# GpSimd sums the squares, wider openings and half-slot splits in a six-stage TensorE kernel

## The reference

```
h = rms_norm(x) * g_pre            # mean over the 1024 channels of x*x
y = layer(h)                       # projections h @ w_in, a mixer, @ w_out
x = x + rms_norm(y) * g_post
```

## Time and profile before

| what | value |
|---|---|
| median of 3 runs | 1914.7 us (1914.07 to 1916.35) |
| span of the profiled execution, first to last instruction | 1915.6 us |
| busy: PE, DVE, ACT, POOL | 1770.9, 926.6, 758.6, 950.2 us |
| mean granted clock of TensorE | 0.966 |
| first product (L660) of the openings of odd, diff, ffn0, ssm, ffn1 | 322.90, 604.13, 880.96, 1256.58, 1527.38 us |

### The profile page before, as it was taken

How to read it: one execution, slowest core, us unless ns; L and a number is a source line. 1 busy time by engine, 2 the same in 40 slices (tenths; PEclk the granted TensorE clock), 3 DMA queues, 4 the chain that set the end, 5 groups by cost and what they waited for, 6 DMA issues and landing times.

```text
span 1915.6 us, 20168 instructions
## 1 busy us (share of the span) xinstructions
PE 1770.9 (92%) x7526; PEld 1337.8 (70%) x7526; DVE 926.6 (48%) x1394; ACT 758.6 (40%) x1261; POOL 950.2 (50%) x1108
## 2 busy tenths in 40 slices
PE   9999989999989889789999999998889899999996
PEld 6766557677767666466888888865445678888885
DVE  2043435666836799526632413357547544032344
ACT  4264554365464324644332322343333542222231
POOL 4433124457944454024655556569124456565662
PEclk9999999999999999799999999999879999999998
DMA  5221112222102221012322332311001223333231
GB/s 201 86 64 61 33 45 87 66 67 77 56 23 88 66 77 56 2 54 89 95 94 97 100 99 93 97 54 55 11 12 33 67 69 96 99 99 98 90 99 66
DMA packets 39697, 139.90 MB, mean 73 GB/s; under 512 B 4528, under 2 KB 4656, under 8 KB 39472
## 3 DMA queue, kind: packets, MB, share of 16 engines
q1 hardware_dynamic: 39600, 138.61, 22.6%
HBM read 136.50 MB, written 2.10 MB: 72 GB/s over the span
## 4 chain that ended last, share of the span: by engine, by line
PE 76%; DVE 11%; ACT 7%; POOL 3%; issue 2%; DMA 0%; SPq 0%; ACTq 0%; DVEq 0%; POOLq 0%
PE ps L643 18%; PE ps L645 17%; PE ps L644 17%; DVE ps L1882 2%; PE ps L706 2%; PE ps L683 2%; POOL wl L2811 2%; PE ps L685 2%; PE ps L684 2%; PE ps L663 1%; PE ps L669 1%; PE ps L660 1%; PE ps L1281 1%; PE ps L959 1%; ACT wh L741 1%
## 5 line engine op out<-in xcount | busy, mean ns | idle before, releaser
L2811 POOL TENSOR_TENSOR wl<-raw,wh 128x256 fp32r<-128x256 f32 x988 | 813.6, 854 | 842.0 <-ACT wh L741 836.3
L741 ACT ACTIVATE wh<-raw 128x1024 fp32r<-128x1024 f32 x246 | 259.9, 1057 | 559.2 <-PE ps L645 499.8
L643 PE MATMUL ps<-hh,wh 128*128 128x512 f32 x1068 | 437.2, 409 | 13.7 <-POOL wl L2811 3.6
L645 PE MATMUL ps<-hh,wl 128*128 128x512 f32 x1068 | 418.7, 392 | 0.0
L644 PE MATMUL ps<-hl,wh 128*128 128x512 f32 x1068 | 418.6, 392 | 0.0
L643 PE MATMUL ps<-mh,wh 128*128 128x512 f32 x632 | 261.7, 414 | 19.2 <-DVE ml L1910 4.0
L643 PEld LDWEIGHTS ps<-hh,wh 128*128 128x128 f32 x1068 | 202.4, 190 | 71.7 <-issue 13.6
L645 PE MATMUL ps<-mh,wl 128*128 128x512 f32 x632 | 250.4, 396 | 0.0
L644 PE MATMUL ps<-ml,wh 128*128 128x512 f32 x632 | 250.0, 396 | 0.0
L644 PEld LDWEIGHTS ps<-hl,wh 128*128 128x128 f32 x1068 | 202.7, 190 | 45.6 <-issue 6.0
L645 PEld LDWEIGHTS ps<-hh,wl 128*128 128x128 f32 x1068 | 202.0, 189 | 43.0
(11 more groups left out here) (477 smaller groups left out, 2443.2 us busy)
## 6 DMA issues: line engine op xcount, KB each, us to landing
raw<-in_w SPq DMA_DIRECT2D x246, 512.0 KB, 3.5
x<-in_x SPq DMA_DIRECT2D x8, 256.0 KB, 7.5
out<-x SPq DMA_DIRECT2D x8, 256.0 KB, 2.0
arena<-in_rope SPq DMA_DIRECT2D x3, 512.0 KB, 3.9
arena<-in_dec SPq DMA_DIRECT2D x1, 1024.0 KB, 7.7
mats<-in_mats SPq DMA_DIRECT2D x1, 576.0 KB, 8.5
raw<-in_w SPq DMA_DIRECT2D x2, 256.0 KB, 3.8
arena<-in_lw SPq DMA_DIRECT2D x1, 512.0 KB, 4.0
```

The source lines that it names most:

```text
L643: e.matmul(ps[b][:], a, xh, start=first, stop=False)
L645: e.matmul(ps[b][:], l, xh, start=False, stop=final).then_inc(pe.sem, pe.up(*step))
L741: e.activation(wh[:, n % NHL, :], raw[:, n % NRAW, :], ACT.Copy).then_inc(rounded.sem, rounded.up(n))
L2811: e.tensor_tensor(wl[:, n % NHL, cut(i, 2)], raw[:, n % NRAW, cut(i, 2)], wh[:, n % NHL, cut(i, 2)].bitcast(F32), SUB).then_inc(split.sem, ...
```

## The change

- `OPENS`: the openings of odd, diff, ffn0, ffn1 and ssm take four groups a block in place of three (two in ssm). The groups that come in no longer stand behind the opening; banks are dealt anew where needed.
- Outside `even`, ACT writes the squares to the eight blocks of `y`, and no longer waits for TensorE. POOL adds squares 1 to 6 onto square 0, one instruction a block (step `sa`). TensorE then needs two float32 matmuls against ones in place of eight, at the end.
- The transposes for `rcol` leave `rs` for a step of their own, `rt`, which stands later in even, odd and diff and nowhere in the other stages. DVE waits for `rb_pre` alone before the steps `e`.
- A slot is split by two POOL instructions of four tiles in place of four of two; the first three slots keep four. Waits by part follow.
- In `odd` `lm` uses the banks 6, 7, 2, 3, `gl` the banks 4, 5, 0, 1; `rt` stands behind gl0. In `diff` e(ub1) and its product `um` stand ahead of the convolution. In `ssm` the two groups su0 and su1 are what is left behind the opening, and the norms stand behind them.

```diff
@@ opening
         out += [("w", g, k) for g in gs]
-        out += [("sq", n) for n in (SQUARES.get(k, ()) if gs == tuple(OPENS["even"]) else (k,))]
-    return out + [("rs",)]
+        if gs == tuple(OPENS["even"]):
+            out += [("sq", n) for n in SQUARES.get(k, ())]
+        elif 1 <= k < KT - 1:
+            out.append(("sa", k))
+    return out + ([] if gs == tuple(OPENS["even"]) else [("sq", KT - 1)]) + [("rs",)]
-OPENS = {"even": [("sq", 0), ("sq", 1), ("sq", 2)], "odd": [("lx", 0), ("lx", 1), ("lx", 2)],
-         "diff": [("ua", 0), ("ub", 0), ("ua", 1)], "ffn0": [("fg", 0), ("fu", 0), ("fg", 1)], "ssm": [("cq", 0), ("cq", 1)]}
+OPENS = {"even": [("sq", 0), ("sq", 1), ("sq", 2)], "odd": [("lx", 0), ("lx", 1), ("lx", 2), ("lx", 3)],
+         "diff": [("ua", 0), ("ub", 0), ("ua", 1), ("ub", 1)], "ffn0": [("fg", 0), ("fu", 0), ("fg", 1), ("fu", 1)],
+         "ssm": [("cq", 0), ("cq", 1), ("ckv", 0), ("kr", 0)]}
@@ steps_odd
-    out += group(lx[3], 8, ("bd", 2), ("lc", 0), ("e", lx[3]), ("bd", 3))
-    out += merge(groups([("gl", j) for j in range(4)], 8, "e", "gm"), lru)
+    gl = groups([("gl", j) for j in range(4)], 8, "e", "gm")
+    out += gl[:8] + [("rt",)] + merge(gl[8:], lru)
@@ steps_diff
-    out = opening(*OPENS["diff"]) + [("e", ("ub", 0)), ("lb",), ("e", ("ua", 0)), ("um", 0), ("e", ("ua", 1)), ("tb",)]
-    out += merge(u[1], conv[:8]) + merge(v, conv[8:34]) + merge(u[2] + u[3], conv[34:78]) + [("le",)]
+    out = opening(*OPENS["diff"]) + [("e", ("ub", 0)), ("lb",), ("e", ("ua", 0)), ("um", 0), ("e", ("ua", 1)), ("tb",),
+                                     ("e", ("ub", 1)), ("um", 1), ("rt",)]
+    out += merge(v, conv[:34]) + merge(u[2] + u[3], conv[34:78]) + [("le",)]
@@ steps_ssm
-    out = opening(*OPENS["ssm"]) + [("an", 0), ("e", c[0]), ("e", c[1])]
-    out += group(c[2], 8, ("e", c[2]), ("nq", 0), ("ns", 0), ("an", 1))
-    out += group(c[3], 8, ("nq", 1), ("e", c[3]), ("nk", 0), ("an", 2))
-    out += group(c[4], 8, ("nk", 1), ("e", c[4]), ("ka", 0))
-    out += group(c[5], 8, ("e", c[5]), ("kb", 0))
+    out = opening(*OPENS["ssm"]) + [("an", 0), ("e", c[0]), ("e", c[1]), ("e", c[2])]
+    out += group(c[4], 8, ("nq", 0), ("ns", 0), ("an", 1), ("nq", 1), ("e", c[3]), ("nk", 0))
+    out += group(c[5], 8, ("nk", 1), ("e", c[4]), ("ka", 0), ("an", 2), ("e", c[5]), ("kb", 0))
@@ pe_norms
+            elif kind == "sq" and stage != "even":
+                claim(e, 7)
+                e.wait_ge(s.pool.sem, s.pool["sa", KT - 2])
+                e.matmul(ps[7][:], M("ones"), y[:, 0, :], start=True, stop=False)
+                e.wait_ge(act.sem, act["square", KT - 1])
+                e.matmul(ps[7][:], M("ones"), y[:, KT - 1, :], start=False, stop=True).then_inc(pe.sem, pe.up("sq", KT - 1))
+                busy[7] = (act, ("rb_pre_ln",))
@@ act_norms, kind "hi"
-                at = square_at(stage)
-                if k >= len(at):
-                    e.wait_ge(pe.sem, pe["sq", k - len(at)])
-                e.activation(at[k % len(at)], x[:, k, :], ACT.Square).then_inc(act.sem, act.up("square", k))
+                if stage == "even" and k >= len(square_at):
+                    e.wait_ge(pe.sem, pe["sq", k - len(square_at)])
+                to = square_at[k % len(square_at)] if stage == "even" else y[:, k, :]
+                e.activation(to, x[:, k, :], ACT.Square).then_inc(act.sem, act.up("square", k))
@@ new
+        def pool_norms(e, stage, step):
+            act, pool = S[stage].act, S[stage].pool
+            if step[0] == "sa":
+                k = step[1]
+                e.wait_ge(act.sem, act["square", k])
+                if k > 1:
+                    e.wait_ge(pool.sem, pool["sa", k - 1])
+                e.tensor_tensor(y[:, 0, :], y[:, 0, :], y[:, k, :], ADD).then_inc(pool.sem, pool.up("sa", k))
@@ split_slot
-            for i in range(0, SLOT, 2):
+            many = parts_of(n)              # 2 for the first three slots, 4 for the others
+            for i in range(0, SLOT, many):
@@ pool_program
                     if (stage, step) in STARTS and 0 < STARTS[stage, step] <= NSLOT - NHL:
                         split_slot(e, STARTS[stage, step] + NHL - 1)
+                    pool_norms(e, stage, step)
```

More of the change, by code:

```diff
@@ L165, in steps_even @@
     sq, sk = ([(g, j) for j in range(4)] for g in ("sq", "sk"))
-    out = opening(*OPENS["even"]) + merge(group(sq[3], 8), [("e", g) for g in sq[:3]]) + [("e", sq[3])] + groups(sk, 8, "e")
+    out = opening(*OPENS["even"]) + merge(group(sq[3], 8), [("e", g) for g in sq[:3]]) + [("e", sq[3]), ("rt",)] + groups(sk, 8, "e")
     out += [("t", "sv", k) for k in range(8)] + [("te", "sv", i) for i in range(4)]
@@ L201, in steps_odd @@
     lx = [("lx", j) for j in range(4)]
-    out = opening(*OPENS["odd"]) + [("e", lx[0]), ("e", lx[1]), ("bd", 0), ("bd", 1), ("e", lx[2])]
-    out += group(lx[3], 8, ("bd", 2), ("lc", 0), ("e", lx[3]), ("bd", 3))
+    out = opening(*OPENS["odd"]) + [("e", lx[0]), ("e", lx[1]), ("bd", 0), ("bd", 1), ("e", lx[2]), ("bd", 2), ("lc", 0), ("e", lx[3]),
+                                    ("bd", 3)]
     lru = []
@@ L293, in steps_ffn @@
             elif f == 1:
-                mul = merge(group(u, 8), pend)
+                mul = pend
             else:
@@ L463, in bank, with parts_of @@
     return of[g[-1] % len(of)]
+def parts_of(n):
+    return 2 if n < NHL else 4
 class Signal:
@@ L606, in program @@
         sqr = [nrm[:, 2, :], nrm[:, 3, :]]
-        def square_at(stage):
-            return sqr + [nrm[:, 4, :], nrm[:, 5, :]] if stage == "even" else sqr
+        square_at = sqr + [nrm[:, 4, :], nrm[:, 5, :]]
         rcol = little(4)
@@ L639, in product @@
                     e.wait_ge(split.sem, split["wl", n])
-            elif i % 2 == 0:
-                e.wait_ge(split.sem, split["wl", n] if i + 2 == SLOT else split["part", n, i])
+            elif i % parts_of(n) == 0:
+                e.wait_ge(split.sem, split["wl", n] if i + parts_of(n) == SLOT else split["part", n, i])
             a, l = tile(stage, step)
@@ L666, in open_products @@
                 n, i = divmod(PLACE[stage, step], SLOT)
-                if i % 2 == 0 or (k, g) == (KT - 1, gs[-1]):
-                    e.wait_ge(split.sem, split["wl", n] if i + 2 >= SLOT or (k, g) == (KT - 1, gs[-1]) else split["part", n, i])
+                if i % parts_of(n) == 0 or (k, g) == (KT - 1, gs[-1]):
+                    whole = i + parts_of(n) >= SLOT or (k, g) == (KT - 1, gs[-1])
+                    e.wait_ge(split.sem, split["wl", n] if whole else split["part", n, i])
                 e.matmul(ps[bank(stage, g)][:], tile(stage, step)[1], hh[:, k, :], start=False, stop=(k == KT - 1)).then_inc(
@@ L696, in pe_norms @@
             pe, dve, act = s.pe, s.dve, s.act
-            if kind == "sq":
+            if kind == "sa":
+                pass
+            elif kind == "sq" and stage != "even":
[5 more added lines that the diff above has]
+                busy[7] = (act, ("rb_pre_ln",))
+            elif kind == "sq":
                 k = step[1]
@@ L700, in pe_norms @@
                     claim(e, 7)
-                    if stage == "even":
-                        e.wait_ge(s_mats, 16)
-                if stage == "even" and k == KT - 1:
+                    e.wait_ge(s_mats, 16)
+                if k == KT - 1:
                     e.wait_ge(consts.sem, consts[EXACT[-1]])
                 e.wait_ge(act.sem, act["square", k])
-                e.matmul(ps[7][:], M("ones"), square_at(stage)[k % len(square_at(stage))], start=(k == 0), stop=(k == KT - 1)).then_inc(
+                e.matmul(ps[7][:], M("ones"), square_at[k % len(square_at)], start=(k == 0), stop=(k == KT - 1)).then_inc(
                     pe.sem, pe.up("sq", k))
+                if k == KT - 1:
+                    busy[7] = (act, ("rb_pre_ln",))
             elif kind == "rs":
+                pass
+            elif kind == "rt":
+                claim(e, 7)
                 e.wait_ge(act.sem, act["rb_pre"])
@@ L808, in dve_norms @@
             elif kind == "rs":
+                e.wait_ge(act.sem, act["rb_pre"])
+            elif kind == "rt":
                 e.wait_ge(pe.sem, pe["rcol"])
                 e.tensor_copy(rcol, fours(ps[7][:])[:, :, 0]).then_inc(dve.sem, dve.up("rcol"))
-                e.wait_ge(act.sem, act["rb_pre"])
             elif kind == "oe":
@@ L1557, in act_odd @@
                     e.wait_ge(pe.sem, pe["lm", j, i])
-                    e.activation((rr, ig)[i][:, j, :], ps[4 + (2 * j + i) % 4][:], ACT.Sigmoid, scale=1.0,
+                    e.activation((rr, ig)[i][:, j, :], ps[LMB[(2 * j + i) % 4]][:], ACT.Sigmoid, scale=1.0,
                                  bias=V(("ba", "bx")[i], j)).then_inc(act.sem, act.up("lm", j, i))
@@ L2807, in split_slot @@
             e.wait_ge(rounded.sem, rounded[n] if n else rounded["half"])
-            for i in range(0, SLOT, 2):
+            many = parts_of(n)
+            for i in range(0, SLOT, many):
```

(5 more changed lines are left out.)

4 lines of the change are left out of this document (2 added, 2 removed), and 8 rows, old and new, of the table BANKS.

## The result

The changed kernel takes 1929.7 us (median of 1928.09, 1929.74 and 1932.09; a fourth run, at 2905 us and a mean granted clock of 0.554, was disturbed and is left out). The kernel before took 1914.4 us beside it: ratio 1.0083, interval [1.0064, 1.0102], 16 us slower. Forecast were 1895 us and a gain of 20 us.

What follows compares the result with a forecast made beforehand. TensorE was taken to bound the kernel, with DVE and POOL limiting the openings; even 1.3, odd 1.3 + 1.7, diff -1.4, ffn0 3.7, ssm 7.0 and ffn1 6.6 sum to 20.2 us, giving 1895 us, range 1881 to 1909.

Steps and rivals of the forecast that it cites:

- Halves: POOL saves 0.6 us a slot; in an ffn worth nothing, in odd 1.7 us gained: Slot splits: two POOL halves at 1.1 us replace 2.83 us; some 10 slots in odd save 6 us, 1.7 counted.
- rival E: Slot splits: a half costs as much as two quarters (1.42 us), p 1.75; 1910 us; chance 0.07.
- they go by turns, one pair in a time p = 1.54: Openings: POOL's 14 wide instructions alternate with DVE's, needing 14 x 1.54 = 21.6 us, plus about 2 us standing still.
- Rival D: Openings: DVE and POOL in turns bound them; p of 2.0 costs 31 us, giving 1926 us; chance 0.07.
- ffn0: Stage ffn0: squares done 3.7 us later than before, yet TensorE gains 3.7 us as the fourth group moves inside.
- ffn1: Stage ffn1: three splits, not four, start before the sixth sum; opening ends at 1552.4, not 1559.0: 6.6 us gained.
- diff: Stage diff: DVE's taps start with the factor 3.7 us later, less 0.3 and about 2 us of waits: loss 1.4 us.
- odd: Stage odd: 4.16 us of DVE's wait and 0.8 for `rcol` go, `rb_pre` comes 3.7 later: 1.3 us gained, halves aside.
- ssm: Stage ssm: two groups go into the opening; the group un starts at 1299.2, not 1306.19: 7.0 us gained.
- even: Stage even: 1.84 us of wait gone, less 0.45 for the transposes further back: 1.3 us gained.
- B: Openings run at TensorE's floor (pairs at 1.2 us or less), end squares waiting for nothing: 38.4 us gained, 1876 us; chance 0.14.
- The wait at 424.50: Odd: TensorE's wait for the chain of DVE's convolutions and LRU, 3.12 us before, should be longer than before.

Runs made afterwards that it cites:

- quarters_again: The changed kernel with every slot split by four POOL instructions again, sums on POOL and wide openings kept: 1916.6 us, ratio 1.0018 to the kernel before.
- wide_openings_alone: The changed kernel with halves and POOL's sums both undone (quarters, squares on TensorE), wide openings kept: 1908.8 us, ratio 0.9973 to the kernel before.
- wide_but_in_diff: Wide openings alone, but diff as in the kernel before (three groups, old order and banks): 1904.4 us, ratio 0.9955 to the kernel before.
- halves_alone: The kernel before with the halves alone: 1931.7 us, ratio 1.0097 to the kernel before.
- combined kernel: Quarters, wide openings but in diff, squares summed by DVE in ffn0, ssm and ffn1: 1900.2 us, ratio 0.9923 to the kernel before.
- eighths_alone: The kernel before with a slot split by eight POOL instructions of 128 columns: 1915.1 us, ratio 1.0009 to the kernel before.
- halves_behind_openings: The kernel before with halves, but quarters for slots that POOL splits during an opening: 1928.1 us, ratio 1.0075 to the kernel before.
- squares_on_pe: The changed kernel without POOL's sums, TensorE doing one square matmul per block, halves and wide openings kept: 1918.8 us, ratio 1.0030 to the kernel before.
- sums_alone: The kernel before with POOL's sums alone (quarters, three groups, two in ssm): 1942.2 us, ratio 1.0154 to the kernel before.

## Why the prediction was wrong

Of the forecast gain of 20.2 us, 1.7 stood for the halves and 18.5 for the openings with their sums. The halves cost 13.1 us in the changed kernel (1929.7 against 1916.6), which is most of its loss. All the rest, measured by quarters_again, lost 3.4 us (1916.6 against 1913.2). So both terms failed: by about 15 us the first, by about 22 us the second. Of these 22 the sums on POOL are 7.8; most of the others are ssm (7.0 forecast, 1.4 with wide openings alone) and ffn1 (6.6 forecast, 2.2).

**Step "Halves: POOL saves 0.6 us a slot; in an ffn worth nothing, in odd 1.7 us gained".** This step failed, and it makes a loss out of the change. POOL's saving is half of what was assumed (a quiet slot takes 2.54 us, against 2.83: a half is 1.27, not 1.1). The other side was not in the sum at all: outside the openings I priced the halves on POOL only, in the forecast and in rival E. There the longer DVE instructions hold TensorE up: in the kernel's time the halves cost 18.5 us alone, 9.9 with wide openings, 13.1 with the sums too. The earlier trace rows had the mechanism in view, I used it for the openings only, and the earlier trace rows had the price of 512 columns.

**Step "they go by turns, one pair in a time p = 1.54".** This was near the mark. POOL's 14 instructions ran from 889.37 to 915.50 with 4.0 us of standing still: (26.1 - 4.0) / 14 = 1.58, where true pairs take 1.6 to 1.7. I took 2 us of standing still. The 2 us missing there and 14 x 0.04 are why the sixth sum ends 31.3 us after the first scaling (915.50 - 884.19) and not 28.7 (907.4 - 878.67). Rival D, which said 1926 us, had p at 2.0 and its point at 1.84: its number came near and its reason was wrong.
The Trainium skill's "SBUF — State Buffer", section "Who interferes with whom", has it that the loser waits for a whole instruction of the other, without sharing bandwidth. The runs agree in that DVE's wait grows with the width of POOL's instruction (0.83, 1.11, 1.66 us), and in the strict turns. I had set the rule aside because a quarter's 0.71 + 0.61 us was more than the 1.11 seen; but 0.71 is the shown duration, and turns of 1.14 us leave POOL 0.53 of them. By the same sum a half has 1.65 - 0.61 = 1.04 us of its 1.27, twice as much for twice the width. So the rule holds if the pair is held for somewhat less than the shown duration; that is an estimate from the spacing, and no run shows the hold itself.

**The sums themselves.** The forecast weighed them against the openings of before, never against wide openings with the squares left on TensorE. By its own numbers those end after 2.3 + 8 x 3.58 = 30.9 us, and with the sums at 30.4: half a microsecond for 30 new instructions. Measured, the last square of ffn0 starts at 30.9 us without the sums and 32.4 with them beside halves, at 30.8 and 32.8 beside quarters; the sums cost 7.8 us beside quarters, 11.0 beside halves, 29 alone.

**Stage by stage.** *ffn0* and *ffn1* were to give 3.7 and 6.6 us, and gave 0.9 and 0.2; wide openings alone give 2.0 and 2.2. In ffn1 three splits did come before the sixth sum, but the first of them began 9.2 us after the first scaling (1544.94 - 1535.74), not 5.2 as in ffn0: the last square starts after 31.6 us, where an end at 27.3 was forecast. *diff*, forecast -1.4, is -5.9: the mechanism (taps on DVE that start late) was right, as wide_but_in_diff shows, and its size too small: the taps start 6.7 us later after the first scaling, not 3.4. *odd*: the 4.16 us of DVE's wait were to pay for the late factor. Wide openings alone gain 1.4 there, within the scatter of that column; with the halves it is a loss of 3.2, with the sums too of 4.2. *ssm*: 7.0 us were to come by the earlier start of un. It came 2.9 us earlier (1307.98 - 1258.97 = 49.0 after the first scaling, before 51.9 by the earlier trace rows), and 8.9 us were lost behind it: 3.7 up to the attention's first scores and 4.3 in the attention (139.9 us from its first scores to its last, before 135.6), which is as long in halves_alone. Nor did an early start of un pay by itself: in wide_openings_alone it comes 4.7 us earlier and the stage gains 1.4. The combined kernel starts it 5.4 us earlier and gains 7.1.

*even*: the mechanism was right; its size, 1.3 us, is below what the even column can tell. At the end of its opening, first the kernel before, then the changed one:

```profile
34.95 0.66 PE L711 MATMUL ps<-mats,nrm 128*128 128x128 f32 x4 [1.44 <-ACT nrm L766]
35.36 0.48 PE L643 MATMUL ps<-hh,wh 128*128 128x512 f32 x1
```

```profile
31.25 1.02 PE L722 MATMUL ps<-nrm,mats 128*128 128x512 f32 x2
31.71 0.79 PE L650 MATMUL ps<-hh,wh 128*128 128x512 f32 x1
```

The product follows the square at once.

**The signs named.** The wait of the end squares for POOL was 0.54 us, neither the 1 us of the forecast nor the nothing of B; TensorE had by then waited 4.9 us for DVE's `hl`, which the forecast did not have. From the first scaling to f = 2's first product it was 32.9 us, not 30.4. DVE's instructions took 1.66 to 1.78 us beside a half, not 1.5, and quiet halves 1.27, not 1.1. The wait at 424.50 grew to 3.67 us, as said. In diff the 5.43 us went, as said, but the wait at 692.52 stayed (2.74, then 2.68 us) and two others came ahead of it. The mark "wrong if ffn0 and ffn1 together give under 6 us" was met.

**Left open.** How much of ssm's loss is a chain, how much the phase in which splits meet DVE's instructions, and how much TensorE's clock (below). Beside wide openings, sums alone or halves alone leave ssm at a gain (2.3 and 1.8), both together lose 6.0; in the kernel before, halves lose 5.3 there and sums 9.8. And odd lies between -3.6 and +0.2 in three kernels whose code is the same there.

## What to carry to other kernels

Price an instruction's width on the engine that shares its operands' memory as well as on its own: fewer, wider instructions on POOL saved it 112 us of work here (halves_alone) and cost DVE 77. Work put on a half-idle engine is not free when its result stands behind that engine's queue and a chain waits for it. And weigh each part against the best kernel without it, not against the kernel before.

## What the runs showed of the hardware

A DVE addition of two SBUF operands (512 columns, 0.69 us) lasts 0.83, 1.11 or 1.66 us beside a POOL instruction of 128, 256 or 512 columns, while DVE instructions with an operand in PSUM stayed at 753 to 754 ns (the taps, L1882) in the kernel before, the changed one, halves_alone and eighths_alone. POOL pays by the instruction: 0.71 becomes 1.14 to 1.19 us at 256 columns, 1.27 becomes 1.6 to 1.7 at 512. In the attention of ssm TensorE's granted clock differs between the kernels. In this stretch of halves_alone (columns as in the earlier trace rows), 150 us behind the stage's first scaling, it was 0.68, between the levels of 1.2 and 2.4 GHz, after 40 us in which TensorE had been busy for 33:

```profile
1412.00:1452.00 40.00, 34.05 (x109) 20.90 (x107) 19.78 (x34) 11.72 (x28) 0.41 (x1) 0.68 0.00 1
```

At the same place the kernel before had 0.73, the changed one 0.67, halves_behind_openings 0.72, and squares_on_pe, which has the halves too, 0.79 after equally 33 us. So halves do not always come with the low clock. The three kernels that lose in ssm by halves (the changed one, halves_alone, halves_behind_openings) are those at or below the clock of the kernel before; sums_alone loses most there, at 0.79. Whether longer waits bring the clock down, or the lower clock makes the stage longer, was not tried by itself.
